# Indexer heads in pairs on the two halves of TensorE, probability copies ahead of exponentials, and masks in nine parts

## What is computed

```python
h = rms_norm(x)                          # prompt and sample rows
a_q, a_k, a_v, i_q, i_k, i_w, b_q, b_k, b_v, m_q, gate = project(h, w_in[l], pos)
# the indexer: 4 heads of 64 values
dots = einsum('bqhd,bld->bqhl', i_q, i_k)
score = einsum('bqh,bqhl->bql', i_w, relu(dots)) * IDX_SCALE
idx = top_k(where(admissible, score, -inf), 256)
# group A: 8 heads over 2 key heads, softmax over the picked keys only
# group B: 4 heads over a window of 128, with a learned sink per head
# group M: 4 heads over 256 memory rows
x = x + (concat(o_a, o_b, o_m) * silu(gate)) @ w_out[l]
```

## Time and profile before

| | |
|---|---|
| median of 3 runs | 1627.69 us (1621.57 to 1631.33) |
| the profiled execution's own time | 1629.99 us |
| its span | 1628.2 us |
| mean granted TensorE clock | 0.941 |
| PE busy | 1440.5 us (88%) |
| DVE busy | 903.0 us (55%) |
| ACT busy | 653.2 us (40%) |

### The profile page before, as it was taken

One profiled execution on the slowest core, in us unless ns is written; L12 is line 12 of the kernel. 1 busy time (PEld: TensorE's weight loads), 2 busy tenths in 40 slices (PEclk: granted clock), 3 DMA queues, 4 the chain that ended last, 5 costly groups with the idle time before them and its releaser, 6 DMA issues. The chain is left out here.

```text
span 1628.2 us, 19386 instructions
## 1 busy us (share of the span) xinstructions
PE 1440.5 (88%) x6364; PEld 794.2 (49%) x6364; DVE 903.0 (55%) x2433; ACT 653.2 (40%) x1627; POOL 161.9 (10%) x191
## 2 busy tenths in 40 slices
PE   5999999999868999988699999999995899998882
PEld 3444465666534444443444445566663444544450
DVE  1444627887635676754133453488773457676533
ACT  1133427775614434333112342477665233333322
POOL 1100013300001000000010001132000001000003
PEclk9999799999979999999689997999998999999976
DMA  6101400213142211101241013003312412211106
GB/s 196 52 25 34 159 26 1 104 41 92 53 98 72 78 53 52 49 11 29 67 153 49 25 39 136 26 1 117 75 57 52 131 53 59 53 52 46 33 4 242
DMA packets 122760, 109.65 MB, mean 67 GB/s; under 512 B 56656, under 2 KB 95280, under 8 KB 122672
## 3 DMA queue, kind: packets, MB, share of 16 engines
q1 hardware_dynamic: 122672, 108.51, 22.0%
HBM read 82.81 MB, written 25.78 MB: 67 GB/s over the span
## 5 line engine op out<-in xcount | busy, mean ns | idle before, releaser
L739 PE MATMUL score_ps<-w_slot,hT 128*128 128x512 f32 (+2 forms) x1024 | 388.2, 538 | 7.4 <-DMA w_slot<-in_w_in_dram 5.0
L739 PEld LDWEIGHTS score_ps<-w_slot,hT 128*128 128x128 f32 x1024 | 195.8, 194 | 188.0 <-issue 181.9
L739 PE MATMUL score_ps<-w_slot,work 128*128 128x512 f32 x512 | 240.1, 624 | 25.7 <-issue 25.7
L1103 ACT ACTIVATE hT<-hT,neg_top 128x128 f32<-128x128 f32 (+8 forms) x144 | 116.8, 813 | 321.3 <-DVE neg_top L1375 321.1
L1257 DVE TENSOR_SCALAR_CACHE_REDUCE work<-bias,trial 128x384 f32<-128x384 f32 (+3 forms) x256 | 226.1, 883 | 6.9
L965 ACT ACTIVATE work<-bias,neg_trial 128x768 bf16<-128x768 f32 (+2 forms) x192 | 198.4, 1043 | 67.1 <-DVE neg_trial L1253 67.1
L739 PEld LDWEIGHTS score_ps<-w_slot,work 128*128 128x128 f32 x512 | 99.5, 200 | 154.7 <-issue 154.5
L810 PE MATMUL score_ps<-hT,w_slot 128*128 128x352 f32 x448 | 135.2, 460 | 1.4 <-ACT gate_raw L1087 1.4
L1158 POOL TENSOR_TENSOR work<-work,norm_sb 128x512 f32<-128x512 f32 (+1 forms) x36 | 43.1, 1197 | 882.4 <-DMA norm_sb<-norm_scratch 882.4
L724 PE MATMUL turn_ps<-ident,hT 128*128 128x128 f32 (+1 forms) x720 | 98.1, 276 | 26.6 <-ACT work L1128 18.4
L869 PE MATMUL score_ps<-akT,query_mem 64*128 64x512 f32 (+4 forms) x448 | 105.8, 560 | 8.0 <-ACT prob_bm L1117 6.7
(11 more groups left out here) (181 smaller groups left out, 1744.9 us busy)
## 6 DMA issues: line engine op xcount, KB each, us to landing
w_slot<-in_w_in_dram SPq DMA_DIRECT2D x8, 2048.0 KB, 10.0
gate_raw<-in_x_prompt_dram SPq DMA_DIRECT2D x16, 512.0 KB, 3.7
work<-gate_scratch SPq DMA_DIRECT2D x16, 512.0 KB, 4.7
norm_sb<-norm_scratch SPq DMA_DIRECT2D x64, 128.0 KB, 3.3
x_scratch<-gate_raw SPq DMA_DIRECT2D x16, 512.0 KB, 3.7
gate_raw<-x_scratch SPq DMA_DIRECT2D x16, 512.0 KB, 3.7
gate_scratch<-gate_raw SPq DMA_DIRECT2D x16, 264.0 KB, 3.1
gate_scratch<-gate_raw SPq DMA_DIRECT2D x8, 528.0 KB, 2.7
```

The source lines that it names most:

```text
L739: last = nc.tensor.matmul(out[:, 0:cols], lhs(k), w[:, k, 0:cols], start=(k == 0), stop=(k == KD - 1))
L1103: ins = nc.scalar.activation(p, p, ACT.Exp, bias=neg, scale=SM_SCALE, accum_out=sums[t % 2][0:r, col:col + 1])
```

## The change

Three edits. (1) **Indexer.** A step is now INDEX(t, pair, c): two heads, one in each half of the partitions, over 512 keys. PE issues two matmuls of up to 512 columns into the two banks of one score buffer. ACT makes two activations, DVE two sums. The sample has three chunks, the last of 32 keys; `out_bm_ps` and its semaphore are no longer used. (2) **ACT's order.** `scalar_order` takes the exponentials of A and of B (not M, nor B of the sample) out of the list where they stand and puts them behind the next run of PT steps. (3) **Masks and OUT.** The mask is nine parts of one step each; parts 0 and 1 (only tiles 5 to 7) stand behind pairs of PT, parts up to 5 under the first half of OUT, parts 6 to 8 under the second. From tile 1 on the second half of OUT stands in front of the first M group.

```diff
-OUT_AT = [[("A", 0, 1), ("A", 1, 0)], [("A", 0, 1)]]
+OUT_AT = [[("A", 0, 1), ("M", 0, 0)], [("A", 0, 1)]]
+def mask_parts(t):
+    return list(range(0 if t in BY_ACT else 3, 9))
...
+        if it[1] == "B" and t and t + 1 in SEARCHED:
+            masks = [("MASK", SEARCHED.index(t + 1), k) for k in mask_parts(t + 1)]
...
                 steps.append(("OUT", t - 1, c))
-                if t + 1 in SEARCHED:
-                    steps.append(("MASK", SEARCHED.index(t + 1), c))
+                while masks and (c or masks[0][2] < 6):
+                    steps.append(masks.pop(0))
                 steps.append(("ADD", t - 1, c))
...
                 held.clear()
+                if masks and masks[0][2] < 3:
+                    steps.append(masks.pop(0))
...
+def scalar_order(steps):
+    order, scores, last = [], [], None
+    for s in steps:
+        if last == "PT" != s[0]:
+            order += scores
+            scores = []
+        if s[0] == "QK" and s[1] and not reads_scores(ITEMS[s[1]]):
+            scores.append(s)
+        else:
+            order.append(s)
+        last = s[0]
+    return order + scores
...
+def index_steps(t):
+    return [("INDEX", t, hp, c) for hp in range(IDX_HEADS // 2) for c in range(-(-NKEYS[t] // 512))]
...
-        index = [("INDEX", t - 2, h) for h in range(IDX_HEADS) if t - 2 in SEARCHED]
+        index = index_steps(t - 2) if t - 2 in SEARCHED else []
...
-    steps += [("INDEX", NT - 1, h) for h in range(IDX_HEADS)] + [("KEYS_T", SMP)]
+    steps += index_steps(NT - 1) + [("KEYS_T", SMP)]
+    last = index_steps(SMP)
     for h, filler in enumerate([("QUERIES", 0), ("MEM", 0), ("MEM", 1)]):
-        steps += [filler, ("INDEX", SMP, h)]
-    steps.append(("INDEX", SMP, IDX_HEADS - 1))
+        steps += [filler] + last[2 * h:2 * h + 2]
```

On the engines:

```diff
 PE, INDEX
-                            q = iqT[half:half + HD, h // 2, t * P:t * P + r]
-                            for c in range(0, NKEYS[t], 512):
...
-                                last = nc.tensor.matmul(o, q, ikT[half:half + HD, k0 + c:k0 + c + w],
-                                                        start=True, stop=True)
+                            for u in range(2):
+                                half = slice(HD * u, HD * (u + 1))
+                                last = nc.tensor.matmul(out[0:r, 512 * u:512 * u + w],
+                                                        iqT[half, hp, t * P:t * P + r],
+                                                        ikT[half, k0:k0 + w], start=True, stop=True)
 ACT
-                    for step in STEPS:
+                    for step in scalar_order(STEPS):
 ACT, INDEX
-                            ins = nc.scalar.activation(relu[0:r, 0:min(n, 1024)], ps[0:r, 0:min(n, 1024)],
-                                                       ACT.Relu, scale=scale)
+                            for k in range(2):
+                                at = slice(512 * k, 512 * k + w)
+                                ins = nc.scalar.activation(index_relu[u % 2][0:r, at], ps[0:r, at], ACT.Relu,
+                                                           scale=iw_abs[0:r, t, 2 * hp + k:2 * hp + k + 1])
                             ins.then_inc(free, 1)
 DVE, INDEX
+                            for k in range(2):
+                                rl = index_relu[u % 2][0:r, 512 * k:512 * k + w]
...
+                                signal(ins, score_added, 2 * u + k + 1)
 DVE, MASK
-                            (need_of_tile, mask_tile)[step[2]](step[1])
+                            mask_part(*step[1:])
```

More of the change, by code:

```diff
@@ L101, in ends_scores @@
     return ITEMS[i][1] != "A" or j % chunks_of(i) == chunks_of(i) - 1
+def mask_parts(t):
+    return list(range(0 if t in BY_ACT else 3, 9))
 def attention_steps():
-    steps, late, waiting, held, last_mixes = [], [], [], [], []
+    steps, late, waiting, held, last_mixes, masks = [], [], [], [], [], []
     last_group = (len(ITEMS) - 1, len(groups_of(ITEMS[-1])) - 1)
@@ L240 @@
 SCORE_USE, TURN_USE, ATT_GROUP = numbered(STEPS)
+INDEX_STEPS = [s for s in STEPS if s[0] == "INDEX"]
 QK_DONE = [s[1:] for s in STEPS if s[0] == "QK" and ends_scores(*s[1:])]
@@ L386, in hybrid_stream_kernel @@
         score_added = sem("score_added")
-        extra_free = sem("extra_free")
         trial_ready = sem("trial_ready")
@@ L1222, in need_of_tile @@
                             link(nc.vector.tensor_tensor(v, v, low, ALU.add))
[L1223 to L1241, removed]
@@ new lines, in mask_part @@
+                        elif k == 3:
+                            link(nc.vector.tensor_scalar(rank, x, v, None, ALU.is_gt, ALU.add,
+                                                         accum_out=count[0:r, i:i + 1]))
+                            link(nc.vector.tensor_scalar(need[0:r, i:i + 1], count[0:r, i:i + 1], -1.0, float(TOPK),
+                                                         ALU.mult, ALU.add))
+                        elif k == 4:
+                            link(nc.vector.tensor_scalar(equal, x, v, None, ALU.is_equal))
+                        elif k == 5:
+                            link(nc.vector.tensor_tensor_scan(rank, one[0:r, 0:1].broadcast_to([r, n]), equal, 0.0,
+                                                              ALU.mult, ALU.add))
+                        elif k == 6:
+                            link(nc.vector.scalar_tensor_tensor(out=equal, in0=rank, scalar=need[0:r, i:i + 1], in1=equal,
+                                                                op0=ALU.is_le, op1=ALU.mult))
+                        elif k == 7:
+                            link(nc.vector.scalar_tensor_tensor(out=equal, in0=x, scalar=v, in1=equal,
+                                                                op0=ALU.is_gt, op1=ALU.add))
+                        else:
+                            link(nc.vector.tensor_scalar(x, equal, 1.0, -NEG, ALU.subtract, ALU.mult))
@@ L1323, in _ @@
[L1323 to L1332 removed]
+                            t, hp, c = step[1:]
@@ L1333, in _ @@
+                            if hp == IDX_HEADS // 2 - 1 and 512 * c + w == n and t < SMP:
+                                link(nc.vector.memset(s[0:CHUNK, w - CHUNK:w], NEG))
                         elif kind == "TOPK":
+                            for b in range(2):
+                                dve.wait_ge(kv_stored[b], 16 * kv_dmas(b, TILES))
                             for t in range(TILES):
```

66 lines of the change are left out of this document (23 added, 43 removed).

## The result

The changed kernel takes 1644.35 us (median of 4, 1642.28 to 1646.3); the kernel before, run beside it, 1627.77. The ratio is 1.0101, 95% interval 1.0067 to 1.0134. The forecast was 1604, faster. The profiled execution took 1642.28 us for a span of 1640.5; before it was 1629.99.

What follows compares the result with a forecast made beforehand. PE, busy 88% of the span, was taken as the bound. 6.4 us from the indexer and 18 from attention made 24.4: 1605.6 for the profiled run, about 1604 for the median, range 1582 to 1626.

Steps and rivals of the forecast that it cites:

- part 3: Masks and OUT in attention: the mask was already hidden, so a loss of 0.9 us a layer, bounds 0 and -5.
- Part 2, the gain: Attention: copies ahead of A's exponentials cut PE's 23.2 us of waits by at most 14.6, taken as 10.5 a layer.
- the six places behind M: Attention: copies behind M's four exponentials, which are not moved, wait 10.9 us; these begin earlier by 2.4 in all.
- Part 2, the loss: Attention, the item starting with A0: later exponentials still fit, since PE has some 2.8 us of other work, ACT needs 2.3.
- Rival C: Attention: exponentials late behind two copies, some 2 us at each of 14 items a layer; slower, 1662 us; chance 0.06.
- the sample's end: Attention of the sample: its copies gain but its last exponentials come later, a loss of 0.6 us.
- Part 1: Indexer pairs: PE works 38 us less in both layers, but only 6.4 us reach the end of the passes.
- the pass of tile 2: Keys with the indexer: later sums on DVE delay NORM's write, so this pass grows from 6.86 to 8.0 us.
- the terms of the sum: Layer 0 gains: tiles 2 and 3 -1.2 each, tile 4 0, tile 5 +0.3, tiles 6 and 7 3.9, sample +1.2.
- the rule of the Trainium skill: Indexer on PE: up to 2x for a contraction of at most 64, so 41 to 20 us a layer.
- Rival A: Indexer: ACT and DVE keep up, all 38 us arrive, with 18 from attention; 1574 us, half of it 1593; chance 0.12.
- A lower clock ..., which nothing here foresees: Sign of a wrong forecast: a lower clock in either stretch, keys with the indexer or attention; no size given.

Runs made afterwards that it cites:

- m2: Kernel before with the second half of OUT early and, in tiles 1 to 3, the reciprocal of A's sums ahead of it: 1633.62 us, ratio 1.0071.
- o4: Kernel before with ACT's new order, M's exponentials also held back behind A0's in tiles 2 to 7, and early second half of OUT: 1628.90 us, ratio 1.0034.
- p2: Kernel before with ACT's new order alone; masks and OUT where they were: 1615.44 us, ratio 0.9946.
- o2: Kernel before with ACT's new order, the exponentials held back issued ahead of M's: 1602.09 us, ratio 0.9826.
- o3: Kernel before with ACT's new order, M's exponentials held back too in tiles 2 to 7, behind A0's: 1577.54 us, ratio 0.9708.
- p1: Kernel before with the indexer's pairs and TOPK's moved wait alone: 1625.57 us, ratio 1.0001.
- n0: Kernel before, whole heads, with only DVE's sums of a pass's first two indexer steps behind its writes of NORM and KEYS_T: 1616.51 us, ratio 0.9955.
- n1: Kernel before with the indexer's pairs and DVE's sums of a pass's first two steps behind its writes of NORM and KEYS_T: 1596.04 us, ratio 0.9799.
- u3: Changed kernel with its third edit undone, the mask in two parts and OUT in its old place: 1614.64 us, ratio 0.9943.
- s1: Changed kernel with the reciprocal of A's sums ahead of the early second half of OUT in tiles 1 to 3: 1636.86 us, ratio 1.0044.
- p3: Kernel before with the nine mask parts and the early second half of OUT alone, ACT's order as before: 1655.69 us, ratio 1.0187.
- m1: Kernel before with the early second half of OUT alone, the mask in its two parts: 1654.58 us, ratio 1.0190.

## Why the prediction was wrong

- **The step that failed most is part 3** ("I take -0.9 a layer in all, bounds 0 and -5"). It followed the mask, found DVE's cover, and never asked what the moved OUT itself had covered; early OUT alone costs 31 us. The text named the other side of it, for the first tile: "the end is set by the DMAs of the reciprocals". The same chain starts in each tile at SCALE, and SCALE stood in the list a few steps ahead of the OUT that was moved. The row of MIX at 499.32 us, 3.64 us behind POOL in the kernel before, says that in tile 2 it was late already. m2 shows 19 of the 31 us to be this chain, o4 that early OUT costs more still in a faster kernel. The cause of the remaining 12 us stays open. In the sum, part 3 was 1.8 us for both layers; alone it measured 30 us, and taken out of the changed kernel 26.
- **Part 2, the gain.** Forecast 10.5 us a layer with waits for copies at some 10 us; p2 has 8.7 us of them, and o2, which has the gain without the loss named next, is 28 us faster than the kernel before (18 to 39 by its interval). Against the 19.8 of the forecast (10.5 less 0.6 at the sample, twice) this term was right, and if anything small. That the six places behind M would stay, 10.9 us, was right as well (o2 has these six, and a seventh at the sample; o3 removes them).
- **Part 2, the loss.** The prediction said "nearest is the item that starts with A0, where PE has some 2.8 us of other work ... and ACT needs 2.3". The place was found, the price was wrong. M's four exponentials, which the text itself said "are not moved", get in between: from 607.62 us on 1.8 us for them and 0.6 for a copy come first. Rival C's mechanism is real, at one item of a tile rather than at each: 8.7 us a layer. The 8.8 us of p2 are what is left of o2's 28; the 19 between them are these waits in two layers and what the clock took behind them, and o2 shows that the overtaking alone was the fault.
- **Part 2, what the trace hides.** In p2's trace attention is 10.2 us shorter than in that of the kernel before, and 10.3 in layer 1, yet only 8.8 us arrive. The profiled run of the kernel before was itself 6.5 us above the median of the runs beside p2, and QUERIES(1) came 4.4 us later in p2 with the same instructions. One term of the sum was also too small: from OUT(7, 0) to OUT(7, 1) p2 needs 28.2 and 28.3 us in its two layers, against 24.8 to 26.6 in before, p1, n0 and n1, where the prediction had 0.6 for the sample's end.
- **Part 1.** The pair's time (two times 512 columns from 121.69 to 122.75 in p1, 1.06 us), the pass of tile 2 (8.30 us, forecast 8.0), the wait for hT (1.88, forecast 1.5 to 2.5) and QUERIES(0) after the last NORM (16.94, forecast 17.9) came as said; two passes lost more than forecast (tile 3 takes 9.0 us in place of 7.4, and tile 4, forecast at 0, 9.2 in place of 7.7). The 6.4 us became 0. In layer 0 the terms of the sum, read from the changed kernel's trace, are -1.4, -1.6, -1.4, +0.3, +4.8 and +1.0 us, together 1.7 in place of 3.0. What the sum had at nothing is the work between the passes: behind the new waits the two projections of keys took 14.1 and 14.5 us in place of 13.2, and QUERIES(0) 12.7 in place of 12.2. That is 2.7 us, more than the passes gave. The lower clock costs some 10 us of this stretch as before, but it now stands behind waits that the change made. (A smaller slip: ACT got 20 more instructions a layer, not 24.) By the rule of the Trainium skill (TensorEngine Tiling, Theoretical Speedup), as the prediction read it, PE would work some 20 us less a layer; the trace says 15.4, where the prediction's own rows had made it 19.
- **Rival A** ("PE's saving comes through") was the right place to look and needed one thing that the change lacks: with DVE's order n1 gains 33 us, against its 38. Of these the order alone gives 7 (n0), so the pairs are worth some 25 on top of it.
- **"A lower clock ..., which nothing here foresees"**: the earlier trace rows did. It showed the clock down behind one wait of 2.14 us, and the forecast added such waits in six passes a layer.
- The chance of slower, 0.07, held one mechanism, C. Part 3 had no rival at all, though between u3 (0.9943) and the changed kernel (1.0101) it makes 26 us.

## What to carry to other kernels

Before moving a long block of work, list every chain that was in flight while it ran, not only the work that is moved under it: 7 us of matmuls covered a way over DRAM that takes 17. When an order is made by holding some instructions back, look for those of the same engine that are not held back and now overtake them. If a stage's engine is the bound and gets less work, the saving arrives only when the instructions that free its buffers stand early enough on the other engines; with that the indexer's pairs and the order gave 33 us here, and the pairs without it nothing.

## What the chip showed that was not expected

- The write of the reciprocals (4 KB) and the read behind it lie some 11 us apart from issue to issue: 11.1 at 488.80 above and in s1's tiles 1 and 2 (489.59 to 500.69, 520.64 to 531.74), and 8.8 to 11.8 over all such pairs of s1's tiles 1 to 7. For the sample, with fewer rows, it is 3.5 and 3.7 us. The read of 128 KB then lands in 3.0 us (median of 28, in the kernel after).
- A wait of 2 us doesn't settle what the clock does. In the kernel before, 2.33 us of waiting at 530.77 left the granted clock at 1.00. In n0_sums_only, with the same instructions around, 1.96 us at 526.91 are followed by 0.50 (1.2 GHz) from 528 to 531 us, with PE busy. In p2, 2.04 us at this place and 0.75 more at 533.59 are followed by 0.50 from 534 to 536. p2 has six such drops behind its first OUT, in tiles 1 to 6, and each takes 1.4 to 1.7 us; o3, with hardly a wait, has one at the first OUT (2.0 us) and then none in 260 us. Fewer waits gave fewer drops; which wait brings one isn't known from these runs.
- With the same instructions up to there, QUERIES(1) came at 232.18 (p3), 232.21 (before), 233.27 (o2), 233.41 (m1), 236.56 (p2) and 236.57 us (o3). A difference of 4 us in this stage between two single traces says nothing; the work at the full clock and the waits are what can be compared.
